# A two-part transformer kernel on one core: the first mixer's input product multiplies the first half of the features for six of its nine column groups before it needs the second half

## What is computed

```python
c_act = jax.nn.silu(c)
mod = c_act @ w_ada[l] + b_ada[l]                       # 2048 x 12288 matrix
sh1, sc1, gt1, sh2, sc2, gt2 = jnp.split(mod[:, None, :], 6, axis=-1)
h = rmsnorm(x, g_mix[l]) * (1.0 + sc1) + sh1
x = x + gt1 * hybrid_mixer(h, ...)                      # z = h @ w_in, three branches, y @ w_out
h = rmsnorm(x, g_ffn[l]) * (1.0 + sc2) + sh2
x = x + gt2 * conv_glu_ffn(h, ...)
```

## Time and profile before

| | us |
|---|---|
| three runs | 3321.6, 3325.29, 3330.5, median 3325.29 |
| the profiled execution: its own time | 3335.25 |
| its span | 3333.6 |
| PE busy | 3221.1 (97%) |
| PEld busy | 3147.8 (94%) |
| DVE busy | 2223.1 (67%) |
| ACT busy | 1420.1 (43%) |

### The profile page before, as it was taken

One profiled execution on the slowest core, in us unless ns is written; L12 is line 12 of the kernel. 1 busy time (PEld: TensorE's weight loads), 2 busy tenths in 40 slices (PEclk: granted clock), 3 DMA queues, 4 the chain that ended last, 5 costly groups with the idle time before them and its releaser, 6 DMA issues.

```text
span 3333.6 us, 62992 instructions
## 1 busy us (share of the span) xinstructions
PE 3221.1 (97%) x27070; PEld 3147.8 (94%) x27070; DVE 2223.1 (67%) x2257; ACT 1420.1 (43%) x1384; POOL 157.7 (5%) x292
## 2 busy tenths in 40 slices
...
GB/s 385 283 306 314 286 275 222 238 205 202 221 206 202 220 164 159 136 159 166 190 197 189 191 197 190 191 197 168 151 140 157 185 193 197 189 191 197 191 191 137
DMA packets 320747, 681.66 MB, mean 204 GB/s; under 512 B 14768, under 2 KB 21620, under 8 KB 320164
## 3 DMA queue, kind: packets, MB, share of 16 engines
...
...
## 4 chain that ended last, share of the span: by engine, by line
PE 86%; DVE 7%; DMA 3%; issue 2%; ACT 1%; POOL 0%; ACTq 0%; DVEq 0%; POOLq 0%; SPq 0%
PE G L695 53%; PE Dn L695 33%; DVE ada_acc L1393 1%; DVE w_lo L1266 1%; PE Dn L698 1%; DMA ada_raw<-in_w_ada 1%; DMA raw<-in_w_in 1%; DMA zT<-in_w_ada 1%; DMA raw<-in_w_out 1%; DVE sq L1317 1%; ACT w_hi L2223 1%; DVE sq L1993 0%; DMA ada_x<-in_w_ada 0%; PE G L698 0%; DVE sq L1333 0%
## 5 line engine op out<-in xcount | busy, mean ns | idle before, releaser
L2223 ACT CAST w_hi<-raw 128x2048 fp32r<-128x2048 f32 (+2 forms) x536 | 1017.5, 1900 | 1418.3 <-DMA raw<-in_w_down 425.6
L1266 DVE TENSOR_TENSOR w_lo<-raw,w_hi 128x2048 fp32r<-128x2048 f32 (+2 forms) x536 | 1218.8, 2274 | 565.1 <-ACT w_hi L2223 564.2
L695 PE MATMUL G<-h_hi,w_hi 128*128 128x256 f32 x5632 | 1579.5, 280 | 13.6 <-DVE w_lo L1266 9.4
L695 PE MATMUL G<-h_lo,w_hi 128*128 128x256 f32 x5632 | 1568.2, 278 | 0.0
L695 PE MATMUL G<-h_hi,w_lo 128*128 128x256 f32 x5632 | 1567.8, 278 | 0.0
L695 PEld LDWEIGHTS G<-h_hi,w_hi 128*128 128x128 f32 x5632 | 1067.7, 190 | 28.6 <-issue 24.4
L695 PEld LDWEIGHTS G<-h_lo,w_hi 128*128 128x128 f32 x5632 | 1067.6, 190 | 0.3
L695 PEld LDWEIGHTS G<-h_hi,w_lo 128*128 128x128 f32 x5632 | 1067.5, 190 | 0.0
L695 PE MATMUL Dn<-act_hi,w_hi 128*128 128x256 f32 x2752 | 763.2, 277 | 7.4 <-DVE act_lo L1811 7.4
L695 PE MATMUL Dn<-act_hi,w_lo 128*128 128x256 f32 x2752 | 762.6, 277 | 0.0
L695 PE MATMUL Dn<-act_lo,w_hi 128*128 128x256 f32 x2752 | 762.5, 277 | 0.0
...
## 6 DMA issues: line engine op xcount, KB each, us to landing
raw<-in_w_up SPq DMA_DIRECT2D x128, 1024.0 KB, 5.4
raw<-in_w_down SPq DMA_DIRECT2D x128, 1024.0 KB, 4.9
...
```

The source lines that it names most:

```text
L695: return nc.tensor.matmul(o, lhsT, rhs, start=start, stop=stop, skip_group_check=True)
L1266: v.tensor_tensor(w_lo[j][:, 0:m], raw[j][:, 0:PIECE_K * n], w_hi[j][:, 0:m], ALU.subtract).then_inc(lo_done, 1)
L2223: s.copy(w_hi[j][:, 0:PIECE_K * n], raw[j][:, 0:PIECE_K * n]).then_inc(hi_done, 1)
```

## The change

The order of the w_in pieces is new. Pieces 0 to 11 are the first-half pieces (j = 0, 1) of groups 5, 6, 3, 1, 2, 0 (`HALF1`); from piece 12 on come the rest, group by group. The sums of groups 1, 2 and 0 wait in PSUM for their second half (group 0 in Dn0). Those of groups 5, 6 and 3 (`PARTED`) are copied to SBUF by ACT (`part1`), and DVE adds them to the second half's sum (`final`), which replaces ACT's copy of these groups. The second half of h is now needed by piece 12 and not by piece 4. Temporaries, PSUM tiles and counts follow from that (`TMP`, `ADA_OUT`, `w_use`). The steps of the mixer are hung on later pieces, `ADA_AT` has no tile before piece 12, and `replicate` moves from pieces 40 to 47 to pieces 60 to 67, in the feed-forward part.

```diff
-ORDER1 = [(0, 0), (0, 1), (1, 0), (1, 1), (0, 2), (0, 3), (1, 2), (1, 3)] + [(g, j) for g in range(2, 9) for j in range(4)]
+HALF1 = [5, 6, 3, 1, 2, 0]
+ORDER1 = [(g, j) for g in HALF1 for j in (0, 1)] \
+    + [(g, j) for g in range(9) for j in ((2, 3) if g in HALF1 else range(4))]
+HALF_AT = 2 * len(HALF1)
+PARTED = (3, 5, 6)
+PART_USE = {5: (0, 0), 6: (1, 0), 3: (0, 1)}
...
-ADA_AT = [0, 0, 0, 0, 3, 0, 2, 2, 1, 0, 1, 2, 2, 2, 3, 2, 2, 3, 2, 3, 0, 2, 0, 1, 4, 3, 3, 2, 3, 2,
-          4, 3, 2, 2, 1, 4, 3, 4, 4, 1, 2, 0, 1, 3, 1, 2, 2, 1, 3, 1, 2, 0]
+ADA_AT = [0, 0, 0, 0, 0, 0, 0, 0, 0, 0, 0, 0, 3, 3, 3, 2, 2, 2, 3, 2, 2, 3, 3, 2, 3, 2, 2, 2, 2, 1,
+          1, 2, 3, 3, 3, 3, 2, 3, 2, 3, 2, 3, 2, 3, 2, 3, 3, 3, 3, 3, 2, 0]
...
-ADA_PE = [[], [3, 6, 9, 12, 15], [3, 8, 13], [2, 5, 8, 11]]
+ADA_PE = [[], [3, 6, 9, 12, 15], [3, 8, 13], [7, 10, 13, 15]]
```

On PE:

```diff
-            for p, t in enumerate(ADA_PE[2]):
+            for p, t in zip((1, 3, 5), ADA_PE[2]):
                 hook(p, ada_direct, 2, t)
-            hook(3, ada_total, 2)
-            for t in ADA_PE[3]:
-                hook(3, ada_direct, 3, t)
-            hook(3, ada_total, 3)
+            hook(7, ada_total, 2)
+            for p, t in zip((9, 10, 11, 11), ADA_PE[3]):
+                hook(p, ada_direct, 3, t)
+            hook(11, ada_total, 3)
...
             for b in range(4):
-                hook(11 + b, lru_gates, b)
-            hook(23, pool_map)
+                hook(18 + b, lru_gates, b)
+            hook(30, pool_map)
```

On DVE:

```diff
+            def final(g):
+
+                b, use = USE1[g]
+                dve.wait_ge(pe_done, LAST1[g])
+                dve.wait_ge(z_evac, g)
...
+                elif g == 5:
+                    i = v.tensor_tensor(zT[:, Z_K:Z_K + 4, :], G[b][:, :, :], PART[g], ALU.add)
...
-            hook(0, ada_late, 29, 33)
-            hook(1, ada_late, 33, 37)
-            hook(2, ada_late, 37, 41)
-            hook(3, second_half)
+            for p in range(10):
+                if p == 8:
+                    hook(p, second_scale)
+                hook(p, ada_late, 29 + 2 * p, 31 + 2 * p)
+            hook(10, ada_late, 49, 51)
+            hook(11, second_half)
...
-            for p, k in ((8, 2), (9, 1), (10, 0)):
+            hook(14, forget_1)
+            hook(16, forget_2)
+            hook(17, forget_series, (15, 13, 11), True)
...
+            for p, k in ((15, 2), (16, 1), (17, 0)):
                 hook(p, conv, k)
...
+            for g in PARTED:
+                hook(LAST1[g], final, g)
...
+            hook(30, pool_2)
+            hook(30, blank_future)
+            hook(30, forget_mask, 0)
```

On ACT:

```diff
-            for n in range(REP):
-                hook(40 + n, replicate, n)
...
+                    if n >= 16 - REP:
+                        replicate(n - 16 + REP)
```

More of the change, by code:

```diff
@@ L959, in _ @@
                         misc_open("f")
-                    else:
-                        pe.wait_ge(n_lo, j + 1)
-                    tiles = [(MISC, 0, True)] + [(G[b][:, f, :], 8 + P * f, f % 2 == 0) for f in range(4)]
-                if j == 0 and use:
-                    pe.wait_ge(g_free[b], use)
+                    tiles = [(MISC, 0, True)] + [(buf[:, f, :], 8 + P * f, f % 2 == 0) for f in range(4)]
+                elif first:
+                    b, use = PART_USE[g] if g in PARTED and j == 0 else USE1[g]
+                    if use:
+                        pe.wait_ge(g_free[b], use)
+                if g in PARTED and j < 2:
+                    buf = G[PART_USE[g][0]]
                 if z0 >= Z_V:
-                    piece_tok(p // 4, p % 4, G[b], 4 * j, j == 0, j == 3)
+                    piece_tok(p // 4, p % 4, buf, 4 * j, first, last)
                 else:
-                    piece(p // 4, p % 4, G[b], h_hi, h_lo, 4 * j, j == 0, j == 3, n, tiles, misc_tile=(g == 0),
+                    piece(p // 4, p % 4, buf, h_hi, h_lo, 4 * j, first, last, n, tiles, misc_tile=(g == 0),
                           call=0 if p == 0 else None)
@@ L972, in _ @@
                 for f in range(4):
-                    b, use = g1_use(len(IN1) + 4 * half + f)
+                    b, use = w_use(4 * half + f)
                     for i, k0 in enumerate(kts):
@@ L1425, in mod_read_first @@
                 dve.wait_ge(ada_sum, i + 1)
-                step(v.tensor_tensor(mod[:, 8 * half:8 * half + 8], Dn[0][:, 2 * (i % 2), 0:8],
+                step(v.tensor_tensor(mod[:, 8 * half:8 * half + 8], ADA_OUT[i][:, 0:8],
                                      cols[:, 8 * half:8 * half + 8], ALU.add))
@@ L1516, in second_half @@
                 scale_first(1)
[L1517 removed]
+            def second_half():
+                ada_first(51, 52)
                 mod_read_first(3)
@@ L1759, in _ @@
                 for f in range(4):
-                    b, _ = g1_use(len(IN1) + 4 * half + f)
+                    b, _ = w_use(4 * half + f)
                     e = 4 * len(IN1) + 8 * half + 2 * f + 1
@@ L2306, in replicate, with part1 @@
                     .then_inc(scr_stored, 16)
+            def part1(g):
+                b, use = PART_USE[g]
+                act.wait_ge(pe_done, PART1[g])
+                if g == 6:
+                    i = s.activation(PART[g], G[b][:, :, :], ACT.Copy, scale=float(P) ** -0.5)
+                else:
+                    i = s.copy(PART[g][:, :, :], G[b][:, :, :])
+                i.then_inc(g_free[b], 1)
             def evac1(g):
-                b, _ = g1_use(g)
+                src = group_buf(g)
```

127 lines of the change are left out of this document (72 added, 55 removed).

## The result

The changed kernel takes **3354.0 us** (median of four runs, 3349.7 to 3356.9) against 3325.2 before: ratio 1.0084, 95% interval 1.0065 to 1.0103. It is 28.8 us slower; the forecast was 3320 with a range up to 3333. Measured a second time it took 3351.1 us, ratio 1.0071 (1.0049 to 1.0094).

The account below looks back on a forecast made before the run. The mixer was taken to run near three limits at once: PE, DVE and DMA. Terms -13.1 + 6.4 - 1.5 + 3 = -5.2 us, taken from the median 3325.3, gave 3320 us, range 3305 to 3333.

Parts of the forecast that it names:

- First stretch: From piece 0 to the start of piece 12: early pieces fill PE's hole, 95.7 us instead of 108.8, gain 13.1.
- Second stretch: Pieces 12 to 30: DVE work moved behind piece 12 makes it 141.7 us instead of 135.3, loss 6.4.
- DVE becomes the bound here: Pieces 12 to 30: DVE's load rises by 17.3 to 132.8 us, above PE's 126.3.
- the handover: End of piece 30: PE's scores and pooling map wait for DVE's pooling and mask steps, 8.9 us that can't overlap.
- Third stretch: Piece 31 to the end of 51: more tiles and a column sum, but `replicate` leaves; net gain 1.5 us.
- Replicas leaving: Pieces 40 to 51: without `replicate`, loads land quicker, gain 3.3 us.
- Eight more tiles and a fourth column sum: Piece 31 to 51: tiles add 10.2 us to DVE, still under PE's 156.4; the column sum adds 1.8 to PE.
- Feed-forward: Pieces 60 to 67: `replicate` adds 5.8 MB of DMA traffic and slows loads, loss 3 us, bounds nothing and 10.
- the 13 of the estimate: Pieces 60 to 67: assumed landing time of a load in us, giving 6.0 us a piece, 0.6 too much.
- those named for right: Piece 12 at 170 to 176, piece 31 about 314, DVE over 0.9 busy between, h_lo wait kept, raw landing times.
- those named for wrong: PE idle for loads in pieces 4 to 11, DVE idle over 30 us behind 12, PE idle over 5 in 60 to 70.
- The slower rival: Mixer behind piece 12: DVE's busy share stays 0.854 and 0.781, stretches 155.5 and 187.5 us, +27, 3353; chance 0.10.

Follow-up runs that it names:

- half tiles: Changed kernel with DVE multiplying only half the width of each adaptive tile of pieces 12 to 51, loads and waits kept: 3339.7 us, ratio 1.0041.

## Why the prediction was wrong

- **First stretch: right.** Piece 12 at 170.7 (172.6 said), 14.7 us gained (13.1 said), with the 4.9 us wait for the low part of h ahead of it, and DVE idle for 32 of the 94 us.
- **Second stretch: the step that failed.** DVE's added work was fairly well counted (136.7 us, 132.8 said), but the step "**DVE becomes the bound here**", and with it a stretch as long as DVE's load and one handover, failed. The stretch took 154.1 us, 12.4 more than said, 18.8 more than before, and halving the tiles' work took only 3.7 off it. In its place: over the stretch DVE was idle for 17 us and PE for 21, and at pieces 18 and 30 DVE was behind while PE waited for short DVE steps placed behind others, once through the shared tile MISC. The gap ahead of piece 19 cost 13.5 us over what the gates take alone (1.4) and wasn't in the sum at all, though the moved gates and `ADA_DONE[4]` = 18 were in the change; the handover was in it with 8.9 and measured 14.1, and 8.4 with the steps moved up. How much of this is order and how much is DVE's work at that place is settled in part only: order alone gave back 11 of 22 us in the whole mixer.
- **PE's load was not redone.** The sum set DVE's 132.8 against PE's 126.3 of before. But the two pieces of group 0 that left the first stretch and were counted as gained there stand in the second now, 2.9 us more than the pieces of v that they replace; PE was busy for 133.5 us.
- **Third stretch: two sizes, both too small, that cancel.** Replicas leaving gain 10 to 11 us (3.3 said). Eight more tiles and a fourth column sum cost 12; 1.8 was said, for the column sum on PE, and DVE's 13.5 us of added work were put at nothing because they stayed under PE's busy time. Net loss 1.5 instead of a gain of 1.5. Loads of `raw` do land sooner, in 5.7 to 8.9 us from 430 to 480.
- **Feed-forward: mis-sized.** Loss 8.8 us (3 said, bound 10); loads took 11 to 18 us to land from 560 on, with a median of 14.3, more than the 13 of the estimate. More than half of it came from the shape of the issues (4.9 to 6.5 us).
- **Sum** of the measured parts: -14.7 + 18.8 + 1.5 + 8.8 = +14.4, which is the difference of the spans.
- **Signs.** Of those named for right, the start of piece 12, the wait for h_lo and both landing times came; piece 31 started at 324.8 and not at 314, and DVE's share between them was 0.89, under 0.9. One of those named for wrong came: PE was idle for 11.5 us from piece 52 to the start of piece 69 (over 5 us in pieces 60 to 70 had been named), 6.0 of them in the last wait, for the split of piece 69.
- **The slower rival** named 3353, right to 1 us, from a constant share of DVE, which half tiles refutes. Its second stretch is nearly right (155.5 for 154.1). Its third isn't: its 187.5 us stand for the part without the last 12.8 us, which took 171.7, and its sum of +27 compares with +14.4 between the profiles. A right number from a wrong reason, and by luck. Its words "at places in its program where no other work stands" have it the wrong way round at the two holes: DVE was busy, and PE waited.
